# Moving the low halves of the V stream to VectorE and reordering the closing part of a decoder block

## The reference

```python
h = rmsnorm(x, g_mix); proj = h @ w_in          # q, k, v, f, B, C, xc and two gates
x = x + (sigmoid(g_attn) * (attn @ Wa) + sigmoid(g_conv) * (conv @ Wc)) @ w_out
# PEER: 8 heads x 16 experts of 128*128 for each token
act = gelu(h @ u[ids].T); x = x + (gates * act) @ v[ids]
# closing: a gated per-layer embedding, and the last norm
x = x + sigmoid(rmsnorm(x, g_ple) @ w_ple_gate) * (p @ w_ple_proj)
return rmsnorm(x, g_final)
```

## Time and profile before

| what | value |
|---|---|
| median of 3 executions | 1901.21 us (1898.22 to 1901.27) |
| profiled execution | 1908.34 us, its span 1906.6 us |
| granted TensorE clock, mean | 0.989 |
| TensorE busy | 1849.2 us |
| VectorE busy | 1280.7 us |
| ScalarE busy | 771.5 us |
| GpSimd busy | 1097.5 us |
| moved by DMA | 360.84 MB |

### The profile page before, as it was taken

One profiled execution on the slowest core, in us unless ns is written; L12 is line 12 of the kernel. 1 busy time (PEld: TensorE's weight loads), 2 busy tenths in 40 slices (PEclk: granted clock), 3 DMA queues, 4 the chain that ended last, 5 costly groups with the idle time before them and its releaser, 6 DMA issues.

```text
span 1906.6 us, 23209 instructions
## 1 busy us (share of the span) xinstructions
PE 1849.2 (97%) x8429; PEld 1515.0 (79%) x8429; DVE 1280.7 (67%) x2144; ACT 771.5 (40%) x1226; POOL 1097.5 (58%) x627
## 2 busy tenths in 40 slices
PE   6999999989999999999999999997999999999988
PEld 5777788878888888888888888886888887778877
DVE  6355412447899958988889881014788898788743
ACT  5433322333332334444444443333444444444543
POOL 6333244433345466767767674456788888886540
PEclk9999999989999999999999999998999999999999
DMA  5211132322244435554445555656999999999821
GB/s 190 88 60 63 56 106 93 122 67 88 90 138 144 149 133 177 187 195 176 177 177 187 194 177 182 232 171 212 349 334 362 349 344 339 357 339 365 289 68 45
DMA packets 144498, 360.84 MB, mean 189 GB/s; under 512 B 17408, under 2 KB 66560, under 8 KB 142720
## 3 DMA queue, kind: packets, MB, share of 16 engines
q1 hardware_dynamic: 100464, 232.29, 36.1%
q0 software_dynamic: 22528, 67.19, 9.4%
q10 hardware_dynamic: 21392, 59.87, 8.4%
HBM read 298.44 MB, written 60.82 MB: 188 GB/s over the span
## 4 chain that ended last, share of the span: by engine, by line
PE 87%; POOL 4%; DVE 3%; issue 2%; DMA 2%; ACT 1%; SPq 0%; ACTq 0%; DVEq 0%
PE pair L761 37%; PE pair L569 15%; PE pair L571 14%; PE pair L570 14%; PE pair L786 2%; POOL picked L536 2%; POOL rows L543 1%; DMA raw<-stream 1%; PE pair L665 1%; DVE sparse_sum L1562 1%; DVE wl L1552 1%; PE pair L685 1%; POOL wl L508 1%; PE pair L739 1%; PE pair L842 0%
## 5 line engine op out<-in xcount | busy, mean ns | idle before, releaser
L508 POOL TENSOR_TENSOR wl<-raw,wh 128x1024 fp32r<-128x1024 f32 x259 | 650.7, 2515 | 688.0 <-ACT wh L943 687.5
L943 ACT ACTIVATE wh<-raw 128x1024 fp32r<-128x1024 f32 x339 | 355.6, 1051 | 140.2 <-DMA raw<-stream 85.0
L761 PE MATMUL pair<-hh,wh 128*128 128x512 f32 x1024 | 402.8, 393 | 0.8 <-ACT scores L1098 0.8
L761 PE MATMUL pair<-hl,wh 128*128 128x512 f32 x1024 | 401.0, 392 | 0.0
L761 PE MATMUL pair<-hh,wl 128*128 128x512 f32 x1024 | 399.4, 390 | 0.0
L569 PE MATMUL pair<-wh,act_h 128*128 128x512 f32 x768 | 302.5, 394 | 13.5 <-issue 8.3
L571 PE MATMUL pair<-wh,act_l 128*128 128x512 f32 x768 | 302.2, 393 | 3.2 <-issue 3.1
L570 PE MATMUL pair<-wl,act_h 128*128 128x512 f32 x768 | 301.7, 393 | 1.5 <-issue 1.3
L761 PEld LDWEIGHTS pair<-hh,wl 128*128 128x128 f32 x1024 | 192.2, 188 | 38.9
L761 PEld LDWEIGHTS pair<-hl,wh 128*128 128x128 f32 x1024 | 192.3, 188 | 37.2
L761 PEld LDWEIGHTS pair<-hh,wh 128*128 128x128 f32 x1024 | 192.3, 188 | 35.6 <-ACT scores L1098 1.0
(11 more groups left out here) (232 smaller groups left out, 2585.0 us busy)
## 6 DMA issues: line engine op xcount, KB each, us to landing
raw<-stream SPq DMA_DIRECT2D x338, 512.0 KB
score_dram<-gout ACTq DMA_DIRECT2D x128, 256.0 KB, 2.4
gate_dram<-stage ACTq DMA_DIRECT2D x12, 2048.0 KB, 7.4
gate<-gate_dram SPq DMA_DIRECT2D x16, 1536.0 KB
score_in<-score_dram SPq DMA_DIRECT2D x128, 192.0 KB
x<-xT SPq DMA_DIRECT2D x4, 512.0 KB, 5.5
picked<-score_dram,score_at POOLq DMA_INDIRECT x128
rows<-stream,row_at POOLq DMA_INDIRECT x128
```

Source lines behind the costliest of these rows:

```text
L508: nc.gpsimd.tensor_tensor(wl[:, n % SL, :], raw[:, n % RAW, :], wh[:, n % SL, :].bitcast(F32), ALU.subtract).then_inc(lo_done, 1)
L761: last = nc.tensor.matmul(psum[u % 2][:], w(weights, U_DENSE + u, c), halves[:, c, :], start=c == 0 and which == 0, stop=c == DC - 1 and w ...
L943: nc.scalar.activation(wh[:, n % SL, :], raw[:, n % RAW, :], ACT.Copy).then_inc(hi_done, 1)
```

## The change

`low_by_dve` is now true for all units from `U_V0 + SL` on, so VectorE makes 120 low parts of V instead of 80, and those of the eleven closing units, and GpSimd none of these. GpSimd's list in the V stage holds the reads and the row fetches alone. `LOW_LAG` is 1: in step s VectorE makes the low part of unit U_V0 + 7 + s instead of U_V0 + 6 + s. In the closing part VectorE makes four low parts after `scale2(0)`, four after `copy_x(3)`, and three after `split2(3)`; `split2(1)` comes before `scale2(3)`. ScalarE makes the last four highs before `std_of(3)` instead of after it, and copies the first four embeddings before `high2(2)` and the second four before `high2(3)`. `turn_scaled` increments its semaphore after each four of its eight column blocks, and `split2` and `out` wait for each half apart.

```diff
--- before.py
+++ after.py
@@ -59,7 +59,7 @@
 GATE_BUFS = 2
 SC = 1
 SCORE_BUFS = 6
-LOW_LAG = 2
+LOW_LAG = 1
 ROUTE_U = 32
 TAIL_U = 18
 LAST = 4
@@ -135,7 +135,7 @@
 
 def low_by_dve(n):
 
-    return U_V0 + SL <= n < U_PLE and n % 3 != 0
+    return n >= U_V0 + SL
 
 
 def lows_before(n, by_dve):
@@ -552,14 +552,10 @@
             for k in range(BATCH):
                 pick(k)
             for step in range(NK):
-                if U_V0 + SL + step < N_UNITS:
-                    low(U_V0 + SL + step)
                 for k in picks_at(step):
                     pick(k)
                 for k in rows_at(step):
                     fetch_row(k)
-            for n in range(U_PLE + SL, N_UNITS):
-                low(n)
 
 
         @block.tensor
@@ -836,12 +832,13 @@
                     last = block_values(b, tile)
                 last.then_inc(unit_used, 1)
 
-            def turn_scaled(tile, pair):
+            def turn_scaled(tile, pair, done):
 
                 for c in range(DC):
                     last = nc.tensor.matmul(pairs[pair][:, c * P:(c + 1) * P], xt[tile][:, c * P:(c + 1) * P], scaled[:, tile, :],
                                             start=True, stop=True)
-                return last
+                    if c % 4 == 3:
+                        last.then_inc(done, 1)
 
             def turn2(i):
 
@@ -851,7 +848,7 @@
                     pe.wait_ge(hf2_ready, 2 * (i - 1))
                 elif i == 0:
                     pe.wait_ge(wsplit, NK)
-                turn_scaled(tile, i % 2).then_inc(turned2, 1)
+                turn_scaled(tile, i % 2, turned2)
 
             for tile in range(1, TT):
                 for b in range(NK - LAST, NK):
@@ -919,7 +916,7 @@
                 pe.wait_ge(diag3_ready, i + 1)
                 if i >= 2:
                     pe.wait_ge(out_ready, 2 * (i - 1))
-                turn_scaled(END_ORDER[i], i % 2).then_inc(turned3, 1)
+                turn_scaled(END_ORDER[i], i % 2, turned3)
 
             for half in range(2):
                 for i in range(TT):
@@ -1229,14 +1226,14 @@
             std_of(1)
             std_of(2)
             high2(0)
-            std_of(3)
             for n in range(U_PLE - LAST, U_PLE):
                 next_high(n)
+            std_of(3)
             high2(1)
+            embeddings(0)
             high2(2)
-            embeddings(0)
+            embeddings(1)
             high2(3)
-            embeddings(1)
             act.wait_ge(emb_ready, 2 * TT)
             for n in range(U_PLE, U_GATE):
                 high(n + SL)
@@ -1573,7 +1570,7 @@
                     dve.wait_ge(pick_gelu, batch + 1)
                     part = slice(BATCH * batch, BATCH * (batch + 1))
                     nc.vector.tensor_tensor(pick_w[:, part], picked[:, part], pick_g[:, part], ALU.mult).then_inc(pick_weight, 1)
-                if step >= LOW_LAG and low_by_dve(U_V0 + SL + step - LOW_LAG):
+                if LOW_LAG <= step < NK - SL + LOW_LAG:
                     low(U_V0 + SL + step - LOW_LAG)
                 for k in rows_at(step - ROW_LAG):
                     dve.wait_ge(pick_weight, k // BATCH + 1)
@@ -1601,8 +1598,8 @@
             def split2(i):
 
                 cols = slice(END_ORDER[i] * P, (END_ORDER[i] + 1) * P)
-                dve.wait_ge(turned2, i + 1)
                 for half in range(2):
+                    dve.wait_ge(turned2, 2 * i + half + 1)
                     if i >= 1:
                         dve.wait_ge(hl2_ready, 2 * (i - 1) + half + 1)
                     bank, g = gained(psum[2 * (i % 2) + half], 2, half)
@@ -1614,15 +1611,22 @@
                                             high, ALU.subtract).then_inc(hl2_ready, 1)
 
             scale2(0)
+            for n in range(U_PLE, U_PLE + LAST):
+                low(n)
             copy_x(1)
             scale2(1)
             copy_x(2)
             scale2(2)
             split2(0)
             copy_x(3)
+            for n in range(U_PLE + LAST, U_PLE + SL):
+                low(n)
+            split2(1)
             scale2(3)
-            for i in range(1, TT):
-                split2(i)
+            split2(2)
+            split2(3)
+            for n in range(U_PLE + SL, N_UNITS):
+                low(n)
 
             def scale3(i):
 
@@ -1632,9 +1636,9 @@
 
             def out(i):
 
-                dve.wait_ge(turned3, i + 1)
                 for half in range(2):
                     k = 2 * i + half
+                    dve.wait_ge(turned3, k + 1)
                     if k >= 4:
                         dve.wait_ge(stored[k % 4], 16)
                     bank, g = gained(psum[2 * (i % 2) + half], 3, half)
```

## The result

| | kernel before | changed kernel |
|---|---|---|
| median of 6 executions each | 1900.65 us (1896.89 to 1904.03) | **1868.8 us** (1867.21 to 1870.06) |
| ratio | | **0.9834** (95%: 0.9821 to 0.9847) |
| profiled execution | 1908.34 us | 1867.21 us |

The record doesn't say on which chip these executions and the two first profiles ran.

The account below looks back on a forecast made before the run. TensorE, busy 97%, was taken as the bound, stalling in V because GpSimd's list took 4.35 us a step against 4.08. Gains of 12 + 7.0 + 0.6 = 19.6 us gave 1901.2 - 19.6 = 1881.6 us, range 1874 to 1896.

Parts of the forecast that it names:

- The V term, 12 us: V stage, 1600 to 1720 us: 12 of 13.1 us lost in stalls and lower clock won back; bounds 0 to 13.1.
- GpSimd's 4.35 us a step: V stage: GpSimd's reads, row fetches and lows sum to 4.35 us a step, over TensorE's 4.08, so it falls behind.
- The allowance of 6.5 us against 10.6: V stage: time for a raw load to land before ScalarE waits, 6.5 us with two steps of lag, 10.6 with one.
- The rates: V stage after the change: GpSimd 3.50 us a step, VectorE 3.43, both under TensorE's 4.08.
- The threshold at 4.08 us: V stage: TensorE's full-speed step, 18 products of 0.2265 us; an engine needing more per step falls behind.
- The reserve of 17 us: V stage: GpSimd's head start, 4.3 steps or 17 us, used up in the 280 us to 1600; then TensorE stalls.
- The start, 0: Start of V, 1267 to 1320 us: no change; bounds -8, and +5 if the run of reads lasts longer.
- The closing part, 7.0 + 0.6: After V: 7.0 us from a shorter embedding stall (bounds 4.3 to 7.8), 0.6 from the last output pair running by halves.
- A: Rival, chance 0.22: transfers bound V, a step needing 372 GB/s; the middle loses 8 us; 1889 us.
- B: Rival, chance 0.08: VectorE becomes V's bound, 4.46 us a step with late raw; slower, 1909 us.
- C: Rival, chance 0.07: transfers stay at 347 GB/s, V loses its 13 us, closing gain mostly given back; 1900 us.
- D: Rival, chance 0.08: the start of V gains too, its 8 us; 1873 us.

Follow-up runs that it names:

- e2: Kernel before with all 120 low parts of V on VectorE and a lag of one step instead of two; 1875.07 us, ratio 0.9867.
- e0: Kernel before, unaltered, profiled once more; 1895.38 us.
- e1: Kernel before with all 120 low parts of V on VectorE, lag still two steps; 1900.02 us, ratio 0.9993.
- e3: Kernel before with the lag alone cut to one step, GpSimd keeping its third of the lows; 1897.92 us, ratio 0.9993.
- g1: Kernel before with a lag of one step and GpSimd making every sixth low of V instead of every third; 1876.65 us, ratio 0.9872.
- g2: Kernel before with a lag of one step and GpSimd making every second low of V instead of every third; 1930.08 us, ratio 1.0156.
- a1: Changed kernel, unaltered, run again on chip 2; 1899.7 us, ratio 0.9968 to the kernel before.
- p1: Changed kernel with GpSimd's reads paced by TensorE's steps, first sixteen two a step, rows fetched four steps later; 1869.86 us, ratio 0.9804 to the kernel before.
- d1: p1 with the first sixteen reads issued in one run, on chip 4; 1867.64 us, ratio 0.9831 to the kernel before.
- c3: Changed kernel with split2 and out waiting for the whole transposition, on chip 6; 1899.58 us, ratio 0.9975 to the kernel before.
- d2: Changed kernel with only a wait for TensorE's step added in GpSimd's loop, on chip 4; 1869.66 us, ratio 0.9842 to the kernel before.
- r2: e2 with three raw buffers instead of four; 1898.88 us, ratio 0.9993 to the kernel before.
- r3: e1 without 14 of the 16 gate loads, the first gates used again; 1876.52 us, ratio 0.987 to the kernel before.

## Why the prediction was too high

**The V term, 12 us, measured 24.9** (e2 against the kernel before). This is the term that was mis-sized, by 13 us, and it explains all of the miss of 12.3 and a little over. Two steps of it failed: how large the loss in V was, and what it waited for.
- The size was read from one execution, as if its stalls were those of the median. Its start had cost 16 us; while TensorE stood there GpSimd went on, and 13.4 us were left to lose in the middle (a reading, as said above). e0, without a stall at the start, loses 21.8. The text had the start as a separate term with bounds of its own; the two trade against each other. The prediction moved the gain from a profile 7.1 us above the median to the median unaltered, and the profile's own sum (13.1 and some 15 at the start) would have shown that the median can't hold both in full. That first profile, 1908.34 us, is longer than every execution of the kernel before on chips 15, 7 and 4 (1906.92 at most) and fits those on 6 and 2 (up to 1910.94 and 1909.54); whether it ran on such a chip isn't on record.
- The cause was given as GpSimd's 4.35 us a step, and the shorter lag was priced at nothing. By that e1 should have won the 12 us and e3 nothing. e1 won nothing, and the largest named wait of TensorE from 1320 to 1800 in the trace before, 3.8 us, was for VectorE's lows. That V gained at all hung on the shorter lag as well, which the text had priced at nothing; this was luck. The 75.9 us that ScalarE waited for raw were put down to GpSimd's late lows; they are 122.5 us in e1, where GpSimd has no low of V to be late with. The allowance of 6.5 us against 10.6 was worked out rightly and then not used: a gate table takes 13.5 us to land in e1, and a unit loaded beside it 11.2, more than the 6.5.

**The rates were right**: GpSimd 3.50 forecast, 3.58 measured; VectorE 3.43, 3.48; a low 1.21, a row 1.28. The threshold at 4.08 us holds too: nothing is lost at 3.92 (g1). The reserve of 17 us is right only roughly: over 112 steps g2, at 4.75 a step, should lose 0.67 x 112 - 17 = 58 us and loses 53.7, but e3, at 4.35, should lose 0.27 x 112 - 17 = 13 and loses 23.5.

**The start, 0**: the median bears it out, but by luck. The profile that the prediction read had a stall there. The kernel before (e0) and all variants that were profiled on chips 15, 7 and 4 have none; the changed kernel itself was profiled only on the first chip, without a stall, and on chip 2, with one. On chips 6 and 2 the changed kernel and its variants lose 29 to 31 us there, and the gain shrinks to 7.4 us (1907.14 to 1899.7). The bound of +5 named a run of reads that lasts longer without the lows in it. The traces fit that (45 us in a1, 24 in the first profile of before), but the size is a third: 30.6 us instead of 16.3 is +14. The kernel before is only some 4 to 7 us longer on those chips; that its middle would have lost most of it anyway is argued, as it has no profile there.

**The closing part, 7.0 + 0.6**: measured 83.7 to 77.1 = 6.6 us (e0 against the first profile of the changed kernel), 6.3 between the medians of e2 and the changed kernel, which may have run on different chips. The chain came as worked out: TensorE resumes at 8.36 us (8.6), its stall is 1.89 us (2.3 in the text; its own sum gives 7.9 - 5.8 = 2.1), no new stall follows up to the last transposition, and the tail from the start of that to the end of the last output is 2.78 us instead of 3.38, the 0.6 of the sum. What wasn't won is the 1.0 us for the clock. In the profile of the changed kernel the ten products after the stall take 3.98 us (1796.70 to 1800.68), 0.40 each, not much less than the 0.445 of the earlier trace rows; a1, p1 and d1 slow down likewise. In c3 and d2, with the same stall, they run at full speed, and the gates start 1.6 us earlier. The clock falls after this stall in four of six profiles.

**The rivals.** A, transfers as the bound: DMA gave 379 GB/s over 280 us and 378 over the next 120, above the 372 that a step needs, and TensorE never waited for it. The Trainium skill (SBUF - State Buffer, the table of paths) has about 358 GB/s from HBM; the trace is above that, over 400 us and not only in one window. B, VectorE as the bound: it was busy 85% (238.88 of 280) and its operations became cheaper, not dearer. (By its own terms B turns to slower at 4.39 us a step, (17 + 13.1 + 7.6)/120 over 4.08, not at 4.42.) C, nothing gained in V: V lost nothing in the changed kernel. D, the gain at the start: the lost time there did vanish between the two first profiles, but not through the change, since e0 shows the same. The time that D gave, 1873, is the nearest of all to 1868.8, by a mechanism that isn't there.

Put together, e0 to the changed kernel's first profile is 1895.38 - 1867.21 = 28.2 us, of which V gives 549.0 - 526.9 = 22.1, the closing part 6.6, and what lies ahead of V takes 0.5 back. The rest to 31.9 is that the medians lie 5.3 us (before) and 1.6 us (changed) above these two executions.

## What to carry to other kernels

Before a stall in a profile is priced, see whether the same stall is in a second execution, and whether an earlier stall in the same one has paid for part of it; losses behind a common reserve don't add. Where a waiting engine names a transfer, ask what holds the transfer when the suspected engine is relieved: here two limits of nearly the same height lay behind each other, each part of the change alone was worth nothing, and both together 25 us. And a long run of indirect reads is worth spreading out even where nothing waits for the reads: on chip 2 that was 29.8 us.

## What the runs showed of the hardware that I had not expected

- On two of the five numbered chips (6 and 2) TensorE's instructions start mostly 1.40 to 2.80 us apart for some 30 us, beginning 17 to 19 us after GpSimd starts a gapless run of indirect reads, and are back to normal about 5 us after the run of 45 us ends (4.7 to 5.7); on the others a run of over 60 us does nothing (e1, e2, r2, r3, d2). Pacing the reads cures it (1899.7 to 1869.86 us on chip 2). What of the chip holds the instructions isn't shown.
- One core moved 379 GB/s over 280 us at a DMA share of 1.03.
- What an indirect read costs GpSimd depends on what VectorE is doing when it begins. In the changed kernel, from 1320 to 1780 us, the 122 reads and fetches that begin while VectorE is idle or has an operand in PSUM take 0.94 us in the mean, the 72 that begin during a low 1.57, and the 22 that begin during the adding of a row 1.42; the last two operations read both inputs from SBUF. The read of 1.74 us in the earlier trace rows is one of these: a low of VectorE ran from 1543.48 to 1544.69.
- VectorE's lows fall from 1.625 us in the mean to 1.218 (e1) once GpSimd does no elementwise work in V.
- After one and the same stall of 1.9 us the clock falls in four profiles (granted 0.56 from 1798 to 1801 in that of the changed kernel) and not in two (1.00), which costs 1.6 us.
